# Expert values scaled in place and summed by accumulating PE transposes, in place of products with a diagonal matrix

## The reference, cut to what matters

```python
def apply_experts(args):
    xt, it, gt = args
    act = jax.nn.gelu(jnp.einsum('nd,nhkd->nhk', xt, u_tab[it]), approximate=False)
    return jnp.einsum('nhk,nhkd->nd', gt * act, v_tab[it])
```

## Time and profile before

| | |
|---|---|
| device time, median of 3 runs | 2485.86 us (2484.33 to 2491.89) |
| profiled execution, span from first to last instruction | 2479.3 us |
| PE busy | 2219.9 us (90%) |
| DVE busy | 1662.4 us (67%) |
| ACT busy | 914.7 us (37%) |
| POOL busy | 887.3 us (36%) |
| bytes read and written by DMA | 942.31 MB, of them 805.36 MB expert gathers |
| TensorE clock, mean over the span | 0.986 of full speed |

### The profile page before, as it was taken

How to read it: one execution, slowest core, us unless ns; L and a number is a source line. 1 busy time by engine, 2 the same in 40 slices (tenths; PEclk the granted TensorE clock), 3 DMA queues, 4 the chain that set the end, 5 groups by cost and what they waited for, 6 DMA issues and landing times.

```text
span 2479.3 us, 30019 instructions
## 1 busy us (share of the span) xinstructions
PE 2219.9 (90%) x9846; PEld 1274.3 (51%) x9846; DVE 1662.4 (67%) x3975; ACT 914.7 (37%) x2664; POOL 887.3 (36%) x796
## 2 busy tenths in 40 slices
PE   9989999989898889898989898889999999977776
PEld 7877745545454445554545554445555545523223
DVE  3874576666665677666777666667667767777764
ACT  2232133332443343344443334433344533433232
POOL 0012043444433334333444343244443434344442
PEclk9999999999999999999999999999999999999999
DMA  5421599999999999999999999999999999999996
GB/s 197 133 73 36 197 385 426 426 426 426 426 424 424 422 400 426 424 425 424 409 410 426 425 424 425 387 426 426 425 425 397 409 426 426 425 427 427 427 425 286
DMA packets 151656, 942.31 MB, mean 380 GB/s; under 512 B 16864, under 2 KB 19136, under 8 KB 53072
## 3 DMA queue, kind: packets, MB, share of 16 engines
q0 software_dynamic: 110592, 805.36, 77.4%
q1 hardware_dynamic: 40912, 135.06, 14.1%
HBM read 939.30 MB, written 1.05 MB: 379 GB/s over the span
## 4 chain that ended last, share of the span: by engine, by line
PE 45%; DMA 38%; DVE 8%; ACT 5%; issue 3%; POOL 0%; DVEq 0%; ACTq 0%; POOLq 0%
DMA arena<-in_uv,idx 37%; PE bank L1929 26%; PE bank L371 6%; DVE arena L1957 4%; PE bank L1561 3%; PE bank L1573 2%; ACT arena L1997 1%; PE bank L843 1%; PE bank L866 1%; DMA weights<-in_sb_v 1%; DVE arena L1216 1%; PE bank L602 1%; ACT arena L1985 1%; PE bank L830 1%; ACT arena L1991 0%
## 5 line engine op out<-in xcount | busy, mean ns | idle before, releaser
L1929 PE MATMUL bank<-arena 128*128 128x512 f32 x3072 | 1426.7, 609 | 222.0 <-ACT arena L1997 213.6
L2018 POOL DMA_INDIRECT arena<-in_uv,idx x768 | 859.5, 1119 | 1370.7 <-PE bank L1929 1241.3
L1929 PEld LDWEIGHTS bank<-arena 128*128 128x128 f32 x3072 | 567.1, 193 | 917.3 <-issue 588.1
L1957 DVE CUSTOM_DVE_ANT_0 arena<-arena,h 128x1024 f32<-128x1024 f32 x512 | 627.5, 1226 | 377.5 <-DMA arena<-in_uv,idx 370.9
L1985 ACT ACTIVATE arena<-arena 128x2 f32<-128x2 f32 x384 | 78.1, 203 | 1133.4 <-DVE arena L1957 1133.1
L1957 DVE CUSTOM_DVE_ANT_0 arena<-arena 128x1024 f32<-128x1024 f32 x256 | 313.7, 1226 | 196.7 <-DMA arena<-in_uv,idx 185.9
L371 PEld LDWEIGHTS bank<-xT,weights 128*128 128x128 f32 x1808 | 250.6, 191 | 52.2 <-issue 35.1
L371 PE MATMUL bank<-xT,weights 128*128 128x128 f32 (+2 forms) x1808 | 269.3, 304 | 0.0
L1997 ACT ACTIVATE arena<-const,arena 128x128 f32<-128x128 f32 x768 | 260.5, 386 | 0.0
L1991 ACT ACTIVATE arena<-arena 128x1 f32<-128x1 f32 x768 | 184.9, 288 | 12.6
L1548 ACT ACTIVATE arena<-bank 128x128 f32<-128x128 f32 (+4 forms) x174 | 52.1, 307 | 136.1 <-PE bank L371 54.0
(11 more groups left out here) (333 smaller groups left out, 1884.8 us busy)
## 6 DMA issues: line engine op xcount, KB each, us to landing
weights<-in_w_q SPq DMA_DIRECT2D x42, 512.0 KB, 17.0
weights<-in_w_in SPq DMA_DIRECT2D x38, 512.0 KB
weights<-in_a_fm SPq DMA_DIRECT2D x28, 512.0 KB
arena<-in_uv,idx POOLq DMA_INDIRECT x768
weights<-in_a_out SPq DMA_DIRECT2D x16, 512.0 KB
weights<-in_b_fm SPq DMA_DIRECT2D x16, 512.0 KB
weights<-in_b_out SPq DMA_DIRECT2D x16, 512.0 KB
arena<-in_w_q SPq DMA_DIRECT2D x14, 512.0 KB, 13.0
```

Source lines behind the costliest of these rows:

```text
L1929: ins = nc.tensor.matmul(acc[:, :], diag[:, e % DIAGS, :], ring[:, e % RING, at:at + 512], start=first, stop=last)
L1957: V.tensor_tensor_reduce(out=u, in0=u, in1=x, scale=1.0, scalar=0.0, op0=ALU.mult, op1=ALU.add, accum_out=dots[:, unit % 2, kx:kx + 1]).th ...
L2018: nc.gpsimd.indirect_dma_start(out=ring[:, s, :], out_offset=None, in_=io[f"uv{unit // PH // NT}"], in_offset=bass.IndirectOffsetOnAxis(ap ...
```

## The change

ACT no longer writes diagonals. It multiplies the `v` half of the ring slot by the coefficient in place (128x1024, one instruction for each expert), and signals `scaled`. It no longer waits for `v_used` there; the four diagonal buffers are gone (a `hole` keeps the addresses behind them). PE then puts each 128-column piece of the scaled slot through a transpose (the piece is the stationary operand, the identity moves; `is_transpose=True`) that accumulates in PSUM, eight for each expert. The sums therefore stand transposed: features on partitions, tokens along the row. At the end of a window ACT copies the one accumulator and DVE the other to `sums_fm` in SBUF (at MIX), PE transposes the eight pieces back into two ordinary banks (`sums_tensor`), and DVE adds these to `h`. PE starts the next window after these eight transposes, no longer after DVE's additions.

```diff
--- before.py
+++ after.py
@@ -46,7 +46,6 @@
 
 RING = 8
 GROUP = 2
-DIAGS = 4
 AHEAD = 15
 TOPK_OPS = 30
 
@@ -1407,7 +1406,7 @@
             if m > 1:
                 act.wait_ge(sem(f"ln_mean_{i}"), m - 1)
             elif m == 1:
-                act.wait_ge(sem("peer_added"), 2 * (i + 1))
+                act.wait_ge(sem("peer_added"), i + 1)
             elif i == 0:
                 for half in range(2):
                     act.wait_ge(*banks.emptied(("w_o", i, half)))
@@ -1501,12 +1500,32 @@
         def peer_added(v, w):
 
             i = w % NT
-            v.wait_ge(sem("v_used"), (w + 1) * TILE_EXPERTS)
-            for half, acc in enumerate((acc_lo, acc_hi)):
+            for half in range(2):
+                job = ("peer", w, half)
+                v.wait_ge(*banks.full(job))
                 hs = h[:, i, half * 512:(half + 1) * 512]
-                ins = nc.vector.scalar_tensor_tensor(hs, hs, ALPHA if w >= NT else 1.0, acc[:, :], ALU.mult, ALU.add)
-                ins.then_inc(sem("peer_added"), 1)
-            v.wait_ge(sem("peer_added"), 2 * (w + 1))
+                nc.vector.scalar_tensor_tensor(hs, hs, ALPHA if w >= NT else 1.0, banks.bank(job)[:, :], ALU.mult,
+                                               ALU.add).then_inc(banks.emptied_sem(job), 1)
+            for half in range(2):
+                v.wait_ge(*banks.emptied(("peer", w, half)))
+            nc.vector.memset(small[:, 45:46], 0.0).then_inc(sem("peer_added"), 1)
+            v.wait_ge(sem("peer_added"), w + 1)
+
+        def sums_copy(engine, copy, w, half):
+            acc = (acc_lo, acc_hi)[half]
+            engine.wait_ge(sem("v_used"), (w + 1) * TILE_EXPERTS)
+            copy(sums_fm[:, 4 * half:4 * half + 4, :],
+                 acc[:, :].rearrange("p (a b) -> p a b", a=4)).then_inc(sem(f"sums_out_{half}"), 1)
+
+        def sums_tensor(pe, w):
+            for half in range(2):
+                job = ("peer", w, half)
+                pe.wait_ge(sem(f"sums_out_{half}"), w + 1)
+                pe.wait_ge(*banks.take(job))
+                out = banks.bank(job)
+                for j in range(4):
+                    ins = nc.tensor.transpose(out[:, j * P:(j + 1) * P], sums_fm[:, 4 * half + j, :], ident)
+                ins.then_inc(banks.full_sem(job), 1)
 
         def fm_tensor(pe, m, i, src):
 
@@ -1585,7 +1604,7 @@
         ring = G.take(RING, 2 * D)
         scores_at = G.at
         scores = G.take(NT * PH * 2 * NKEYS)
-        diag = G.take(DIAGS, P)
+        hole = G.take(4, P)
         sc2 = G.take(2, NKEYS)
         cand, cand2, eq = (G.take(PK, PK) for _ in range(3))
         top, topi, posf = (G.take(2, PK) for _ in range(3))
@@ -1638,6 +1657,7 @@
 
         xw = xT.rearrange("p a b -> p (a b)")[:, 0:D].rearrange("p (a b) -> p a b", a=KC)
         norm_junk = G.view(MIX + D, D)
+        sums_fm = G.view(MIX, KC, P)
 
         def cached_home(n, j):
 
@@ -1920,17 +1940,19 @@
             pe.wait_ge(sem("w_o_last_added"), 2)
             for s in range(UNITS // PH * WINDOW):
                 if s and s % WINDOW == 0:
-                    pe.wait_ge(sem("peer_added"), 2 * (s // WINDOW))
+                    sums_tensor(pe, s // WINDOW - 1)
                 for e in range(s * GROUP, (s + 1) * GROUP):
                     first, last = e % TILE_EXPERTS == 0, e % TILE_EXPERTS == TILE_EXPERTS - 1
-                    pe.wait_ge(sem("diag"), e + 1)
-                    for half, acc in enumerate((acc_lo, acc_hi)):
-                        at = D + 512 * half
-                        ins = nc.tensor.matmul(acc[:, :], diag[:, e % DIAGS, :], ring[:, e % RING, at:at + 512],
-                                               start=first, stop=last)
+                    pe.wait_ge(sem("scaled"), e + 1)
+                    for c in range(KC):
+                        acc, at = (acc_lo, acc_hi)[c // 4], D + P * c
+                        ins = nc.tensor.matmul(acc[:, c % 4 * P:(c % 4 + 1) * P], ring[:, e % RING, at:at + P], ident,
+                                               start=first and c % 4 == 0, stop=last, is_transpose=True,
+                                               skip_group_check=True)
                     ins.then_inc(sem("v_used"), 1)
                 beside.run(s)
                 late.run(s)
+            sums_tensor(pe, UNITS // PH - 1)
             beside.run(UNITS * PK)
 
         def stream_vector(v):
@@ -1992,10 +2014,9 @@
                                              scale=gate[:, par, j:j + 1]).then_inc(sem("coef"), 1)
                     for j in range(GROUP):
                         act.wait_ge(sem("coef"), e + j + 1)
-                        if e + j >= DIAGS:
-                            act.wait_ge(sem("v_used"), e + j - DIAGS + 1)
-                        nc.scalar.activation(diag[:, (e + j) % DIAGS, :], ident, ACT.Copy,
-                                             scale=coef[:, par, kx + j:kx + j + 1]).then_inc(sem("diag"), 1)
+                        value = ring[:, (e + j) % RING, D:2 * D]
+                        nc.scalar.activation(value, value, ACT.Copy,
+                                             scale=coef[:, par, kx + j:kx + j + 1]).then_inc(sem("scaled"), 1)
                     beside.run(e // GROUP)
                     late.run(e // GROUP)
                     if kx == 2 * GROUP and unit < UNITS - 1:
@@ -2041,6 +2062,7 @@
             for w in range(6):
                 n, i, base = w // NT + 1, w % NT, WINDOW * (w + 1)
                 yield base
+                sums_copy(v, nc.vector.tensor_copy, w, 1)
                 peer_added(v, w)
                 if n > 1:
                     yield base + 1
@@ -2062,6 +2084,8 @@
             yield from first_scalar(act)
             for w in range(6):
                 n, i, base = w // NT + 1, w % NT, WINDOW * (w + 1)
+                yield base
+                sums_copy(act, nc.scalar.copy, w, 0)
                 yield base + 1
                 norm_squares(act, 2 * n - 1, i)
                 yield base + 2

```

## The result

| | before | after |
|---|---|---|
| median of 20 runs on the same chip, us | 2487.0 (2481.9 to 2492.5) | 2492.3 (2488.9 to 2498.0) |
| ratio, 95% interval | 1 | 1.0024 (1.0015 to 1.0032) |
| profiled span, us | 2479.3 | 2488.1 |
| TensorE's mean granted clock | 0.986 | 0.886 |

The changed kernel is 0.24% slower, 6 us by the ratio, where I had forecast 0.4% less. Lines of its page, against the earlier trace rows; the GB/s line has 40 slices of 62.2 us.

The account below looks back on a forecast made before the run. The prediction took the transfers, at 426 GB/s, as the bound, with only holes to win. Its terms, -12 + 1.8 + 0.6 = -9.6 us against the span of 2479.3 us, gave 2476.3 us as median; range 2467 to 2498.

Parts of the forecast that it names:

- What bounds the kernel: Whole stream: transfers run at their limit, 426 GB/s; only holes in the rate can be won, 21 us of missing transfer.
- PE's sums: PE's value sums: eight transposes an expert, 799 to 1475 us in place of 1426.7, no surcharge for accumulating; PE busy near 1600.
- rival 3: PE's transposes as slow as the products because accumulating costs a second pass: 4.2 us a group, 2490 us; chance 4%.
- ACT: ACT's scaling: 768 passes of 1.14 us replace diagonals, adding 615 us, to 1530 us busy; hidden by transfers in full stretches.
- Window ends, 0 us: Five window ends inside the stream: copies and transposes back cost 1 to 2 us on each engine, covered by the ring.
- 5 x 2 = 10 us if the ring were dry: Window ends inside the stream: the cost if the ring could not cover 2 us at each of five ends.
- 12 of 21 us come back: Holes in the transfer rate: faster PE wins about 3 us in each of three, and 3 behind the weights; bounds 0 and 21.
- The first rival: Holes are not PE's but begin with a reciprocal, weights or attention chains: 0 to 5 us come back, 2486 us; chance 28%.
- ACT becomes the bound: Attention bursts of the sb layer: ACT's longer passes outlast the slots in flight, +25 us, 2511 us (2521 with dry ends); chance 16%.
- The end, +1.8: Kernel's end: passes, transposes, copy and transposes back start the additions 1.1 to 2.8 us later, taken as +1.8 us.
- Instructions, +0.6: Instruction fetching: 3072 more products with as many loads, 43 bytes each, 0.26 MB, +0.6 us at 426 GB/s.
- The clock: PE: more time at 1.2 GHz expected in the last two windows; as a rival, 1.2 GHz throughout, 2790 us, chance 4%.

Follow-up runs that it names:

- old ends: The changed kernel without copies and transposes back at window ends (left out), additions reading the transposed sums as they stand: 0.9991 of the kernel before.
- the copy earlier: The changed kernel with ACT's copy of its accumulator issued one group earlier, ahead of the next window's first two value passes: 1.0002 of the kernel before.
- the later additions: The changed kernel with ACT's copy one group earlier, and DVE's additions to h moved one group later: 1.0004 of the kernel before.
- The ends alone: The changed kernel with ACT making diagonals again, as moving operand against the stationary value piece, window ends as in the change: 1.0014 of the kernel before.

## Why the prediction was wrong

- *What bounds the kernel* was right: nine microseconds more of missing transfer, nine more of span in this pair of traces.
- *PE's sums.* The pace was as said: 16 transposes take 2.13 us at full clock and about 3.5 to 3.7 us at the lower one (2.13 in the end's rows, 3.68 at 685.24). Accumulating costs nothing extra (rival 3 out). The records' 966.6 us are within the 799 to 1475. "PE busy near 1600" was too low (1825.4): the value records are 168 us over the full-clock 799, PE's other work 66 us over its 793, at a mean clock of 0.886 in place of 0.986.
- *ACT.* 1.14 us a pass, measured 1134 ns; busy 1479 in place of 1530 us, as pairs overlap (2.17 us). The size was right. What its length does to an instruction queued behind it was not asked.
- ***Window ends, 0 us*: this step failed.** I had 1 to 2 us on each engine and let the ring cover it. It was 2.8 us to ACT's copy, 3.82 us on DVE, 5.78 us on ACT, and then the norm's own stall on the same ring. Net 8 us (old ends to change), about 5 of them by the copy's place. With the copy earlier the same norm still makes PE wait 4.52 us and POOL 5.55 near 682 us, but the row at 680 holds 397 GB/s in place of 353. I named the wait on `v_used` and what was behind it, but not what was ahead of the copy on its own engine: two passes that the same change had made three times as long. My "5 x 2 = 10 us if the ring were dry" was the right size, by a cruder way: it had no copy behind passes in it.
- ***12 of 21 us come back*: this step failed too.** With the old ends it was 0.09% (2 us, interval from -5 to +1), with the earlier copy nothing. I had seen that PE's 20.00 us of busy time in the first hole were the catching up after a stall, and still priced a shorter catching up at 3 us for each hole. The slots stay away because dots come late or weights do; with PE's sums short and the scaling gone 17.5 us are still missing. The first rival, given 28% and 2486 us, describes the change apart from its ends.
- *ACT becomes the bound*: not in the change, where it is busy 17.94 us of 20 at most in the rows above. But passes together with slow products cost 14 us, the deepest of it at 1920 to 2000 us, the place that this rival had named, so the idea of ACT in the path was half right; PE's saving pays for it.
- *The end, +1.8*: +0.5 us to the additions. The two passes took 2.17 us and not 2.28, PE ran at full clock throughout (the low end of my 1.1 to 2.8), and the first addition starts 0.69 us after the transposes back begin, when four of the eight are done; I had put it behind all eight. The full clock was luck: the trace of the later additions ended at the lower one.
- *Instructions, +0.6*: 0.40 MB more, 0.9 us at 426 GB/s. 6240 records were added, loads included, so some 64 bytes each and not 43. The ends alone give the same: 18528 more, 1.18 MB.
- *The clock.* It fell from 0.986 to 0.886, but the full stretches keep their rate. In the last window, where the value transposes are all that PE does,

```profile
2380.00:2400.00 20.00, 9.50 (x64) 7.84 (x62) 13.67 (x37) 10.45 (x20) 9.94 (x9) 0.91 1.01 425
```

the mean clock is still 0.91 and the rate 425 (the row at 2300 has 0.72, also with 64 transposes alone, and 427). Where others wait for PE the lower clock does count: 1.92 us for the transposes back at 665.99 where the copy earlier has 1.04, and 2.6 us at the end of the later additions. The Trainium skill, "TensorE: Matmul & The Clock Gate", Part 4 (PE-mode transpose), says that a transpose does not count as activity for the clock gate; taken to the letter this row would read 0.5. The trace does not bear that out here: three of its four groups of 16 transposes take 2.13 us, one 3.36.

By the ratio the change takes 2485.86 x 1.0024 = 2491.8 us, inside the range of 2467 to 2498 but on the other side of the kernel before than forecast. Being less than 0.3% away it belongs to the outcomes that I had given 33%.

**What stays open.** Summed over rows of 20 us under 422 GB/s from 320 to 2460 us, the change misses 17.7 us near the five window starts and 12.7 elsewhere; with the old ends it is 2.7 and 22.5. With the copy earlier it is 2.8 and 20.7: 15 us are won at the window starts, and 8 come back elsewhere. Why the other holes are 10 us shallower in the change, whether later stalls find a different ring or it is scatter of one trace, was not settled; in the thirteen other traces they are 16 us or more. Nor which item of VectorE's bursts would have to go for the old holes to close: only the reciprocal was tried, and cutting it left one hole and moved the other.

## What to carry to other kernels

When a change makes an instruction longer, look not only at its own engine's total but at everything that is issued behind it in order and that another engine waits for; here a 0.6 us copy behind two 1.1 us passes, at five places, cost about 5 us in all, and issuing it ahead of them won these back. An engine that is 100% busy in a hole of the transfer rate may only be catching up: remove its work altogether in one experiment before counting on the hole. And take the same kernel's trace twice before reading differences of a few microseconds.

## What had not been expected of the hardware

- 128x128 fp32 products with the value as the stationary side (ends alone) made 12288 records and 1473.7 us busy, against 1426.7 us in 3072 records for the 128x512 form: four times the weight loads cost 3% of PE's busy time.
- ScalarE's pass does not halve with its width: 1134 ns for 1024 columns, 707 ns for 512. By these two, 280 ns are there at any width, an estimate that the 386 ns for 128 columns bear out.
- VectorE's `tensor_scalar` over 128x1024 fp32 in place takes 750 ns where ScalarE takes 1134 ns.
- VectorE's reciprocal takes 4.95 us for 768 columns and 2.55 us for 384, 6 to 7 ns a column, against 0.73 ns for the `tensor_scalar`.
